# Two transformer blocks in one launch: copying the rotated rows of q and k by DMA, and rotating heads 1 to 3 on GpSimd

## The reference

```python
for l in range(2):
    n = rmsnorm(h, attn_norm[l])
    u, v_sgu, q, k, v_att = split(n @ w_in[l])        # widths 512 each
    y_sgu = sgu_mixer(gelu(u), gelu(v_sgu), ...)      # gated mixing over chunks of 128 tokens
    y_att = diff_attention(q, k, v_att, positions, ...)
    h = h + concat([y_sgu, y_att]) @ w_out[l]
    h = h + conv_ffn(rmsnorm(h, ffn_norm[l]), ...)
return rmsnorm(h, final_norm)

def apply_partial_rope(t, cos, sin):                  # t: one half head, 64 wide; the first 16 are rotated
    t1, t2 = t[..., :8], t[..., 8:16]
    rot = concat([t1 * cos - t2 * sin, t2 * cos + t1 * sin])
    return concat([rot, t[..., 16:]])
```

## Time and profile before

| | us |
|---|---|
| median of 3 runs (1813.77 to 1814.24) | 1813.98 |
| span of the profiled execution | 1809.1 |
| what lies around that span, against the median | 4.9 |
| PE busy in the span | 1770.8 (98%) |
| DVE busy | 1123.6 (62%) |
| POOL busy | 987.3 (55%) |
| ACT busy | 780.7 (43%) |

### The profile page before, as it was taken

One profiled execution on the slowest core, in us unless ns is written; L12 is line 12 of the kernel. 1 busy time (PEld: TensorE's weight loads), 2 busy tenths in 40 slices (PEclk: granted clock), 3 DMA queues, 4 the chain that ended last, 5 costly groups with the idle time before them and its releaser, 6 DMA issues. The chain is left out here.

```text
span 1809.1 us, 26088 instructions
## 1 busy us (share of the span) xinstructions
PE 1770.8 (98%) x9009; PEld 1440.2 (80%) x9009; DVE 1123.6 (62%) x1862; ACT 780.7 (43%) x1270; POOL 987.3 (55%) x1228
## 2 busy tenths in 40 slices
PE   8999999999999999999999999999999989999998
PEld 6867888888888886788888888877666778899886
DVE  4777656566656338756666655654486567666665
ACT  5434543333334334443333333456576664333332
POOL 6543445555465543255465564447311558888885
PEclk9999999999999999999999999999999999999999
DMA  7221224443423221122443332413201112223321
GB/s 255 94 94 47 82 75 158 151 147 120 151 93 117 93 93 48 47 105 105 151 162 123 134 125 93 140 50 109 101 2 48 47 47 94 93 95 115 117 94 47
DMA packets 102183, 183.73 MB, mean 102 GB/s; under 512 B 6810, under 2 KB 66892, under 8 KB 100044
## 3 DMA queue, kind: packets, MB, share of 16 engines
q1 hardware_dynamic: 101916, 182.46, 28.7%
q10 hardware_dynamic: 176, 0.07, 0.0%
HBM read 180.42 MB, written 2.10 MB: 101 GB/s over the span
## 5 line engine op out<-in xcount | busy, mean ns | idle before, releaser
L979 POOL TENSOR_TENSOR w_lo<-raw,w_hi 128x256 fp32r<-128x256 f32 (+1 forms) x1124 | 909.8, 843 | 796.6 <-ACT w_hi L1048 793.0
L2460 PE MATMUL ps<-n_hi,w_hi 128*128 128x512 f32 (+1 forms) x1320 | 509.0, 386 | 3.9 <-ACT zc L1351 1.8
L2462 PE MATMUL ps<-n_hi,w_lo 128*128 128x512 f32 (+1 forms) x1320 | 499.7, 379 | 0.0
L2461 PE MATMUL ps<-n_lo,w_hi 128*128 128x512 f32 (+1 forms) x1320 | 499.1, 378 | 0.0
L1048 ACT ACTIVATE w_hi<-raw 128x1024 fp32r<-128x1024 f32 (+2 forms) x331 | 307.7, 937 | 353.1 <-PE ps L2462 235.9
L2460 PEld LDWEIGHTS ps<-n_hi,w_hi 128*128 128x128 f32 x1320 | 248.1, 188 | 54.2 <-issue 7.2
L2461 PEld LDWEIGHTS ps<-n_lo,w_hi 128*128 128x128 f32 x1320 | 248.3, 188 | 47.3 <-issue 2.6
L2462 PEld LDWEIGHTS ps<-n_hi,w_lo 128*128 128x128 f32 x1320 | 247.9, 188 | 47.7
L2004 DVE TENSOR_TENSOR ps<-ps,sq 128x512 f32<-128x512 f32 x88 | 61.3, 699 | 181.3 <-PE ps L2462 178.9
L2460 PE MATMUL ps<-x_hi,w_hi 128*128 128x512 f32 x416 | 167.2, 402 | 0.1
L2462 PE MATMUL ps<-x_hi,w_lo 128*128 128x512 f32 x416 | 162.2, 390 | 0.0
(11 more groups left out here) (357 smaller groups left out, 2639.5 us busy)
## 6 DMA issues: line engine op xcount, KB each, us to landing
raw<-in_w_up SPq DMA_DIRECT2D x44, 1024.0 KB, 6.6
raw<-in_w_ff SPq DMA_DIRECT2D x32, 1024.0 KB, 6.5
raw<-in_w_in SPq DMA_DIRECT2D x26, 1024.0 KB, 6.1
zb<-in_ada_w SPq DMA_DIRECT2D x16, 1536.0 KB, 8.2
raw<-in_w_down SPq DMA_DIRECT2D x44, 512.0 KB, 4.2
raw<-in_w_out SPq DMA_DIRECT2D x12, 1024.0 KB, 6.5
raw<-in_w_in SPq DMA_DIRECT2D x4, 512.0 KB, 8.1
za<-in_x SPq DMA_DIRECT2D x4, 512.0 KB, 6.0
```

Source lines behind the costliest of these rows:

```text
L979: last = pool.tensor_tensor(part[0], part[1], part[2], ALU.subtract)
L2460: pe.matmul(out, l_hi, r_hi, start=start, stop=False)
L2461: pe.matmul(out, l_hi, r_lo, start=False, stop=False)
L2462: return pe.matmul(out, l_lo, r_hi, start=False, stop=stop)
```

## The change

The rotation no longer uses PE. Of each 64-row half head only rows 0 to 15 are rotated; the partner rows (0 to 7 and 8 to 15 exchanged) are now fetched by four DMAs of 8 rows each, from the tile into a buffer `swapped`, whose other rows are zeroed once. The sign moves into the angle: `invf` is negative on the first eight rows. The matrix `rotT` is gone from the constants. Head 0's q and k are still rotated on DVE, from `swapped` instead of PSUM, and the gate products of the mixing come before and between them. Heads 1 to 3 are rotated on POOL, in place, one q or k ahead of each of the low parts of quarters 7 to 12. Head 1's k is projected before the attention steps, whole; heads 2 and 3 follow in steps 0 to 8 by a table, in pieces of 2 to 4 of their eight groups of three matmuls, and the first outs tile is split over steps 9 and 10. The scores of heads 1 to 3 wait for POOL (`rope_set`) instead of DVE.

```diff
-def tile_at(n):
-    return (1 + (n + 2) // 4, (n // 2 + 1) % 2, n % 2) if 0 <= n < 10 else None
-def rope_at(n):
-    return (1 + n // 4, n // 2 % 2) if n % 2 == 0 and n <= 10 else None
+OUT_STEPS = {9: (0, 0, 2), 10: (0, 2, 4), 11: (1, 0, 4), 12: (2, 0, 4), 13: (3, 0, 4), 14: (4, 0, 4),
+             15: (5, 0, 2), 16: (6, 0, 2), 17: (6, 2, 4), 19: (7, 0, 4)}
+TILE_STEPS = {0: [(2, 0, 0, 4)], 1: [(2, 0, 4, 8)], 2: [(2, 1, 0, 4)], 3: [(2, 1, 4, 8)], 4: [(3, 0, 0, 3)],
+              5: [(3, 0, 3, 6)], 6: [(3, 0, 6, 8), (3, 1, 0, 2)], 7: [(3, 1, 2, 5)], 8: [(3, 1, 5, 8)]}
+COPY_AT = {0: (1, 1), 2: (2, 0), 4: (2, 1), 7: (3, 0), 9: (3, 1)}
...
@@ SP
+                def swap_rows(t, j):
+                    n = 8 * l + 2 * t + j
+                    emptied(sp, ("qk"[j], l, t))
+                    if t == 0 and l:
+                        sp.wait_ge(rope_set, 6 * l - 1 + j)
+                    elif t == 1:
+                        sp.wait_ge(swap_read, 2 * l + 1 + j)
+                    elif t:
+                        sp.wait_ge(rope_set, 6 * l + 2 * t + j - 3)
+                    for base in (0, 64):
+                        for to, at in ((base, base + ROT // 2), (base + ROT // 2, base)):
+                            sp.dma_start(swapped[to:to + ROT // 2, n % 2, :], (qT, kT)[j][at:at + ROT // 2, t, :])\
+                                .then_inc(swap_in[n % 2], 16)
                 for i in range(2):
                     load_qk(l, i)
                 load_out("outs", l, 0)
+                if l == 0:
+                    sp.wait_ge(swap_zero, 1)
+                for t in range(2):
+                    for j in range(2):
+                        swap_rows(t, j)
                 load_out("outa", l, HT)
+                for t in range(2, HEADS):
+                    for j in range(2):
+                        swap_rows(t, j)
                 load_up(room(("up", l, 0)), l, 0)
@@ POOL
+            pool.memset(swapped[:, :, :], 0.0).then_inc(swap_zero, 1)
+            def rope(l, t, j):
+                x_ = (qT, kT)[j][:, t, :]
+                n = 8 * l + 2 * t + j
+                k = 2 * (6 * l + 2 * t + j - 2)
+                turned = swapped[:, n % 2, :]
+                if t == 1 and j == 0:
+                    pool.wait_ge(qk_ready, 2 * l + 2)
+                pool.wait_ge(swap_in[n % 2], 64 * (n // 2 + 1))
+                pool.tensor_tensor(x_, x_, cosF, ALU.mult).then_inc(rope_step, 1)
+                pool.tensor_tensor(turned, turned, sinF, ALU.mult).then_inc(rope_step, 1)
+                pool.wait_ge(rope_step, k + 2)
+                pool.tensor_tensor(x_, x_, turned, ALU.add).then_inc(rope_set, 1)
+            rope_before = {STR["qk", l, 0].g0 + 7 + i: (l, 1 + i // 2, i % 2) for l in range(DEPTH) for i in range(6)}
...
+                    if g in rope_before:
+                        rope(*rope_before[g])
                     lo(g, g + 1, g - 3 if g >= 4 else None)
@@ ACT
                 sgu_hi(0)
+                ensure(gqk + 3 + LOOK)
                 sgu_hi(1)
-                ensure(gqk + 3 + LOOK)
+                qk_out(1, 0)
+                ensure(gqk + 4 + LOOK)
                 for n in range(ATT_STEPS):
-                    if (turned := rope_at(n)) is not None:
-                        qk_out(*turned)
-                    if (tile := tile_at(n)) is not None:
+                    if n in COPY_AT:
+                        qk_out(*COPY_AT[n])
+                    for tile in TILE_STEPS.get(n, ()):
                         ensure(gqk + 2 * tile[0] + tile[1] + 1 + LOOK)
@@ DVE
                     x_ = (qT, kT)[j][:, t, :]
                     n = 8 * l + 2 * t + j
-                    if n >= 2:
-                        dve.wait_ge(qk_ready, n - 1)
-                    dve.tensor_tensor(turn[n % 2], filled(dve, ("rope", "qk"[j], l, t))[:, :], sinF, ALU.mult)\
-                        .then_inc(freed(("rope", "qk"[j], l, t)), 1)
+                    dve.wait_ge(swap_in[n % 2], 64 * (n // 2 + 1))
                     emptied(dve, ("qk"[j], l, t))
+                    dve.tensor_tensor(turn[n % 2], swapped[:, n % 2, :], sinF, ALU.mult).then_inc(swap_read, 1)
...
+                sgu_gate(0)
                 rope(0, 0)
+                sgu_gate(1)
                 rope(0, 1)
-                sgu_gate(0)
-                sgu_gate(1)
                 sgu_lo(0)
@@ PE
-                rope(0, 0)
-                mix(0)
-                rope(0, 1)
-                for g in range(1, HT):
+                for g in range(HT):
                     mix(g)
                 project(1, 0)
+                project(1, 1)
...
-                            pe.wait_ge(qk_ready, l * 8 + 2 * hd + 2)
+                            if hd == 0:
+                                pe.wait_ge(qk_ready, 2 * l + 2)
+                            else:
+                                pe.wait_ge(rope_set, 6 * l + 2 * hd)
```

More of the change, by code:

```diff
@@ L81, in constants @@
     half = ROT // 2
-    rot = np.zeros((P, P), np.float32)
     invf = np.zeros((P, 1), np.float32)
@@ L338, in bank_plan @@
         qk(0, 1)
-        b.take(("rope", "q", l, 0), 6)
-        b.take(("rope", "k", l, 0), 7)
         for g in range(HT):
@@ L343, in bank_plan @@
         qk(1, 0)
+        qk(1, 1)
         for n in range(ATT_STEPS):
@@ L354, in bank_plan @@
                 b.take(("O", l, v // 4), 5, counted=False)
-            if (turned := rope_at(n)) is not None:
-                b.take(("rope", "qk"[turned[1]], l, turned[0]), 6 + turned[1])
             if n >= 7 and (n - 7) % 4 == 0 and (n - 7) // 4 < HEADS:
                 b.take(("subsum", l, (n - 7) // 4), 4, counted=False)
-            if (tile := tile_at(n)) is not None and tile[2] == 0:
-                qk(*tile[0:2])
+            for tile in TILE_STEPS.get(n, ()):
+                if tile[2] == 0:
+                    qk(*tile[0:2])
             if n in OUT_AT:
@@ L570, in build @@
         ang_ready, rope_ready = sem("ang_ready"), sem("rope_ready")
+        swap_zero, swap_read, rope_step, rope_set = (sem("swap_zero"), sem("swap_read"), sem("rope_step"),
+                                                     sem("rope_set"))
+        swap_in = [sem(f"swap_in{i}") for i in range(2)]
         lam_dots, lam_exp = sem("lam_dots"), sem("lam_exp")
@@ L1185, in _ @@
                 sgu_hi(0)
+                ensure(gqk + 3 + LOOK)
                 sgu_hi(1)
-                ensure(gqk + 3 + LOOK)
+                qk_out(1, 0)
+                ensure(gqk + 4 + LOOK)
                 for n in range(ATT_STEPS):
-                    if (turned := rope_at(n)) is not None:
-                        qk_out(*turned)
-                    if (tile := tile_at(n)) is not None:
+                    if n in COPY_AT:
+                        qk_out(*COPY_AT[n])
+                    for tile in TILE_STEPS.get(n, ()):
                         ensure(gqk + 2 * tile[0] + tile[1] + 1 + LOOK)
-                    if n in OUT_AT:
-                        ensure(STR["outs", l].g0 + OUT_AT.index(n) // 2 + 1 + LOOK)
+                    if n in OUT_STEPS:
+                        ensure(STR["outs", l].g0 + OUT_STEPS[n][0] // 2 + 1 + LOOK)
                     if n < 16:
@@ L1952, in _ @@
                         emptied(dve, ("subsum", l, hd))
-                    if (turned := rope_at(n)) is not None:
-                        rope(*turned)
                     if n < 2:
@@ L2639, in _, with project @@
                 tokens([("va", l, t) for t in range(NT)], STR["va", l].g0)
-                def project(t, j, halves=(0, 1)):
+                def project(t, j, first=0, end=DT):
                     g = STR["qk", l, 0].g0 + 2 * t + j
@@ L2645, in project @@
                     key = ("qk"[j], l, t)
-                    out = bank(key) if halves[0] == 0 else ps[BK[key][0]]
-                    for k in range(4 * halves[0], 4 * halves[-1] + 4):
+                    out = bank(key) if first == 0 else ps[BK[key][0]]
+                    for k in range(first, end):
                         last = product(out[:, :], wh[:, k * P:(k + 1) * P], wl[:, k * P:(k + 1) * P],
                                        n_hi[:, k, :], n_lo[:, k, :], k == 0, k == DT - 1)
-                    if halves[-1] == 1:
+                    if end == DT:
                         last.then_inc(quarter_done, 1)
-                def rope(t, j):
-                    emptied(pe, ("qk"[j], l, t))
-                    out = bank(("rope", "qk"[j], l, t))
-                    pe.matmul(out[:, :], rotT, (qT, kT)[j][:, t, :], start=True, stop=True)\
-                        .then_inc(full[BK["rope", "qk"[j], l, t][0]], 1)
                 def mix(g):
@@ L2729, in _ @@
                         last.then_inc(pv_done, 1)
-                    if (turned := rope_at(n)) is not None:
-                        rope(*turned)
                     if n == OUT_AT[-1]:
                         out_tile("outs", DT - 1, x_hi, x_lo)
+                    if n == 9:
```

(7 more changed lines are left out.)

28 lines of the change are left out of this document (12 added, 16 removed).

## The result

The changed kernel takes 1817.52 us (median of 18 runs, 1815.18 to 1819.97), the kernel before 1814.76 in the same runs (18, 1812.71 to 1817.47): a ratio of 1.0015, 95% interval 1.0009 to 1.0022. It is slightly slower; 1798.5 was forecast. The profiled span is 1814.8 us, 5.7 more than before. The medians are only 2.8 us apart. The rest comes from the profile of the kernel before: runs that list both show 1.7 to 2.1 us between span and time (1814.8 and 1816.57 for the profiled run of the changed kernel), so its span of 1809.1 belongs to a run of about 1811, under all 18 of these. The 4.9 us of the table before the change are therefore mostly a difference between executions, not something around the span; the forecast, which subtracts from the median, does not hang on it.

A forecast was written before the change was run, and what follows sets the result against it. TensorE, busy 98% of the span, was taken as the bound: 17.3 us removed, less 1.0 for a stall and 0.8 for contention, gives 15.5; span 1793.6 plus 4.9 makes 1798.5 us. Forecast range 1795.5 to 1802; 8 in 10: 1795.0 to 1806.0.

The forecast's parts named there:

- The 4.9 us of the table before the change: Whole kernel before: the runs' median, 1813.98, lies 4.9 us above the profiled span; added to the forecast span.
- Removed from PE: Attention, both layers: 16 rotation matmuls 13.8 us, their waits 1.7, waits before products with V 1.8; 17.3 us saved.
- The order of copies, rotations and weights: SyncE and GpSimd queues around attention: copies and rotations come in time, with 3 to 3.5 us spare.
- The rival of late rotations: GpSimd's rotations before the scores: PE waits up to 4 us a layer, 8 in all; 1806 us; chance 0.14.
- the slower one: GpSimd's in-order queue: rotations waiting for copies hold up weights, PE waits 58 us in all; 1857 us; chance 0.07.
- The new stall of step 6: Attention step 6: ScalarE's split of weight quarter 10 delays later copies; 0.5 us a layer, 1.0 in all.
- Contention on VectorE: Attention: VectorE loses some 16 us to GpSimd; steps that get late cost 0.8 us over both layers.
- a third by the rows: VectorE beside GpSimd: estimated loss of a third of GpSimd's 46 us of rotation instructions, some 16 us.
- the lock's bound: VectorE and GpSimd's common ports: each of 36 GpSimd instructions could hold VectorE for 1.29 us, 23 us a layer.
- The rival of the thin steps: Attention steps 4, 5, 7 to 10: VectorE or ScalarE bounds, PE waits 2 to 3 us/layer; 1803-1805 us; chance 0.10.
- small bounds at their worst: Whole kernel: new stall 2.5 us, late VectorE steps 0.8, twice 1.5 more; 1802 us as the range's upper end.

The follow-up runs named there:

- experiment 1: The changed kernel with GpSimd's three instructions per rotation cut from 512 columns to one, heads 1 to 3 staying unrotated but for one column: 1794.19 us, ratio 0.9903.
- experiment 4: The changed kernel with heads 1 to 3 rotated on VectorE from the copied rows, nothing of it on GpSimd: 1811.20 us, ratio 1.0004.
- experiment 8: The changed kernel with each GpSimd rotation instruction cut into two of 256 columns: 1811.28 us, ratio 0.9968.

## Why the prediction was wrong

**Removed from PE: right.** Without the contention PE is busy 14.2 us less (1770.8 to 1756.6; 13.8 forecast), and the span 16.3 less (17.3 by the medians of the runs). The sum had 17.3, less 1.0 for a stall; that 1.0 is not what makes it meet the 16.3, for the stall did not come.

**The order of copies, rotations and weights: right.** Head 0's copy was used at 100.17 (forecast 99 to 100), the first scores came at 107.90 (108.3), and no scores waited for GpSimd. GpSimd did stand 3.47 us for a copy, that of head 3's q, but nothing on PE waited for it. The rival of late rotations and the slower one, which ran through the same queue, did not happen.

**The new stall of step 6: too large.** No wait over 0.3 us shows there in the changed kernel; 0.5 a layer was taken.

**Contention on VectorE: the step that failed.** The prediction said that "VectorE is no worse off than before on average" and took 0.8 us for steps that get late; experiment 1 measured 22.0. Three things were wrong in it:

- *The size.* What it called a third by the rows was one instruction that lost 0.5 us, times two. VectorE lost 28.8 us in steps 0 to 11 of both layers where 16 were taken; the lock's bound was 46. The one row at hand reads as an instance of the lock, not as a measure of its share.
- *The yardstick.* On average the sentence came true: VectorE is busy 1120.0 us, before 1123.6. But it weighed VectorE's load against the load before, and not against the steps that the change leaves. Before, VectorE had 48.4 us of work in twelve steps of 61.1; now it has 49.2 in steps that PE passes in 49.0. The instructions that are held lie where it counts, the gates and low parts in steps 0 to 2 and the negation ahead of the head copy of step 10, and a wait of 3.08 us needs one late maximum. The rival of the thin steps had this mechanism, and experiment 4 bears it out even without GpSimd; its price of 2 to 3 us a layer was too small, for what was 6.8 in idle time alone (13.6 for both).
- *The clock.* No term and no rival had it. In the two attentions it stood at 1.2 GHz behind some of the waits, and this cost 8.4 us.

So the balance is 16.3 gained, 22.0 given back: 5.7 longer in the profiled span, 2.8 (0.15%) in the runs. One sum of the prediction is off without consequence: its small bounds at their worst add up to 1803, not 1802.

## What to carry to other kernels

Weigh an engine's work in a stretch against that stretch as the change leaves it, not against the work of before. When work moves to GpSimd, list VectorE's instructions beside it and charge those that are held with the rest of the GpSimd instruction in flight, step by step and not on average; short GpSimd instructions make that rest short. Held here were instructions with both inputs in SBUF and multiplications of SBUF rows by a scalar (0.90 us at 121.88 for 256 columns, 0.35 at 139.09), but no reader of PSUM and no reciprocal. A copy that frees an accumulator belongs ahead of work that waits for the same late engine. And price a wait of TensorE at more than its length where the trace shows the clock falling behind it.

## What was not expected of the hardware

Tiny VectorE instructions pay in full: a product of one column took 1.14 us under a rotation (0.16 without), and the negation of two columns up to 1.25 (0.17), while a reciprocal of the same two columns kept 0.15 throughout. And waits of like length were not always followed by the lower clock: products behind the 2.11 us wait of experiment 4 took 0.39 us, those a little behind the 1.94 us of experiment 8 took 0.63. What decides between them stays open.
